# Outer gate tiles of a gated recurrence: the neighbour's three products in one contraction block of 96 rows, and a dot product summed on VectorE

## The reference

```python
xb = xf.reshape(B, L, LRU_BLOCKS, LRU_BLOCK)
r = jax.nn.sigmoid(jnp.einsum('blnc,ncd->blnd', xb, w_a).reshape(B, L, W) + b_a)
i = jax.nn.sigmoid(jnp.einsum('blnc,ncd->blnd', xb, w_x).reshape(B, L, W) + b_x)
log_a = -LRU_C * r * jax.nn.softplus(-lam)
u = jnp.sqrt(-jnp.expm1(2.0 * log_a)) * (i * xf)
```

## Time and profile before

| | us |
|---|---|
| median of three executions (lowest, highest) | 2432.12 (2431.92, 2433.31) |
| the profiled execution's own time | 2431.23 |
| its span, first to last instruction | 2429.4 |
| TensorE busy, share of the span | 2395.8, 99% |
| GpSimd busy | 1727.2, 71% |
| VectorE busy | 1204.4, 50% |
| ScalarE busy | 630.7, 26% |

### The profile page before, as it was taken

How to read it: one execution, slowest core, us unless ns; L and a number is a source line. 1 busy time by engine, 2 the same in 40 slices (tenths; PEclk the granted TensorE clock), 3 DMA queues, 4 the chain that set the end, 5 groups by cost and what they waited for, 6 DMA issues and landing times.

```text
span 2429.4 us, 51213 instructions
## 1 busy us (share of the span) xinstructions
PE 2395.8 (99%) x19460; PEld 2345.1 (97%) x19460; DVE 1204.4 (50%) x1610; ACT 630.7 (26%) x913; POOL 1727.2 (71%) x1970
## 2 busy tenths in 40 slices
PE   7999999999999999999999999999999999999997
PEld 7999999999999999999999999999999999999997
DVE  7665555577754522022366554545786544221222
ACT  2312121326751210011113222221466412100110
POOL 7474757588887777777865756565888877777774
PEclk9999999999999999999999999999999999999998
DMA  5554545322233222322235635453222322223222
GB/s 176 183 187 158 183 155 188 142 96 85 88 100 92 92 92 85 100 86 87 94 130 204 225 140 187 151 183 106 91 92 83 98 97 91 92 84 101 87 86 88
DMA packets 113001, 296.76 MB, mean 122 GB/s; under 512 B 11680, under 2 KB 12448, under 8 KB 112864
## 3 DMA queue, kind: packets, MB, share of 16 engines
q1 hardware_dynamic: 60480, 198.21, 24.9%
q10 hardware_dynamic: 52384, 96.56, 11.4%
HBM read 254.34 MB, written 40.38 MB: 121 GB/s over the span
## 4 chain that ended last, share of the span: by engine, by line
PE 68%; DVE 2%; ACT 1%; DVEq 1%; issue 0%; POOL 0%; ACTq 0%; POOLq 0%
PE banks L395 63%; PE banks L562 1%; PE banks L570 1%; PE banks L531 1%; PE banks L586 1%; PE banks L548 0%; DVE scratch L1095 0%; POOL w_low L381 0%; PE banks L484 0%; DVE ret_acc L1338 0%; DVE scratch L1157 0%; PE banks L442 0%; DVEq L1092 0%; DVE scratch L842 0%; PE banks L540 0%
## 5 line engine op out<-in xcount | busy, mean ns | idle before, releaser
L381 POOL TENSOR_TENSOR w_low<-w_raw,w_high 128x256 fp32r<-128x256 f32 (+1 forms) x1544 | 1285.1, 862 | 61.7
L376 POOL TENSOR_SCALAR w_high<-w_raw 128x1024 fp32r<-128x1024 f32 (+3 forms) x420 | 439.2, 1046 | 619.0 <-PE banks L395 578.0
L395 PE MATMUL banks<-x_high,w_high 128*128 128x260 f32 x4096 | 831.3, 284 | 16.0 <-DVE x_low L749 11.0
L395 PE MATMUL banks<-x_high,w_low 128*128 128x260 f32 x4096 | 825.5, 283 | 0.0
L395 PE MATMUL banks<-x_low,w_high 128*128 128x260 f32 x4096 | 823.5, 283 | 0.0
L395 PEld LDWEIGHTS banks<-x_high,w_high 128*128 128x128 f32 x4096 | 632.2, 189 | 24.5 <-issue 17.0
L395 PEld LDWEIGHTS banks<-x_high,w_low 128*128 128x128 f32 x4096 | 631.3, 188 | 0.0
L395 PEld LDWEIGHTS banks<-x_low,w_high 128*128 128x128 f32 x4096 | 631.0, 188 | 0.0
L395 PE MATMUL banks<-split_scratch,w_high 128*128 128x260 f32 x3776 | 606.9, 282 | 2.1 <-POOL w_low L381 0.9
L395 PEld LDWEIGHTS banks<-split_scratch,w_high 128*128 128x128 f32 x3776 | 517.1, 188 | 3.6 <-ACT split_scratch L1613 1.3
L395 PE MATMUL banks<-split_scratch,w_low 128*128 128x260 f32 x1888 | 380.0, 283 | 0.0
(11 more groups left out here) (170 smaller groups left out, 1926.5 us busy)
## 6 DMA issues: line engine op xcount, KB each, us to landing
w_raw<-in_wstream SPq DMA_DIRECT2D x268, 512.0 KB, 3.5
w_raw<-in_wstream SPq DMA_DIRECT2D x88, 384.0 KB, 3.0
scratch<-in_sret ACTq DMA_DIRECT2D x64, 512.0 KB, 6.8
out_ret_s<-scratch ACTq DMA_DIRECT2D x64, 512.0 KB, 3.5
scratch<-v_rows ACTq DMA_DIRECT2D x64, 256.0 KB, 4.1
w_raw<-in_wstream SPq DMA_DIRECT2D x48, 320.0 KB, 2.8
w_raw<-in_wstream SPq DMA_DIRECT2D x16, 448.0 KB, 3.2
out_ret_p<-scratch ACTq DMA_DIRECT2D x8, 512.0 KB, 2.8
```

What stands on the lines that cost most here:

```text
L376: pool.tensor_scalar(WH[:, j, w], WR[:, j, w], 1.0, 0.0, ALU.mult, ALU.add)
L381: m = pool.tensor_tensor(WL[:, j, p], WR[:, j, p], WH[:, j, p].bitcast(F32), ALU.subtract)
L395: m = pe.matmul(out, wt[:, w, blk * P:(blk + 1) * P], x[xi], start=first and n == 0, stop=last and n == 2)
```

## The change

For outer tiles the neighbour's part of the contraction is at most 32 rows deep (`CR`). ScalarE lays these 32 rows three times into one tile `XS`: high, low, high, 96 rows (`corner`, three copies; one buffer, so it waits for the gates of the outer tile before). The weight block holds the same 32 rows three times, and GpSimd overwrites the third 32 rows of its high part with the low part, so that one block of 96 rows holds high by high, high by low and low by high. TensorE runs it with two matmuls in place of six. The gates wait for `XS` in place of the neighbour tile's low part. GpSimd does this in the second unit of an outer tile, once in each half: drain, copy of 32x128, drain, and the half is reported split only then. In ScalarE's queue the copies stand behind the high part of conv block 3; behind the neighbour copies of turn 0; ahead of the neighbour copies of group 1's tile 1; and behind those of its tile 2.

The dot product's products go into a tile of 16 columns first; a second VectorE instruction adds the two halves into the wide tile, after a drain, and one fp32 matmul is left.

```diff
--- before.py
+++ after.py
@@ -53,6 +53,11 @@
+CR = 32
+OUTER = (0, GT - 1)
...
@@ -151,6 +156,10 @@
 
 
 N_GLX = 2
+
+
+CORNER_UNITS = {B_Y[g][t] + 1 for g in range(GROUPS) for t in OUTER}
+CORNER_BLOCKS = [MT + 2 * w + 1 - YG_UNIT[0] for w in range(2)]
 
 
 PIECE = 2
@@ -202,7 +211,8 @@
         EPST, TOUCH = EPST2[:, 0:1], EPST2[:, 1:2]
         QZ = sb("q_sample", [P, KT, NS * QW])
         VW = sb("v_wide_sb", [P, VT, P])
-        QKW = sb("qk_wide_sb", [P, KT, P])
+        QKW = sb("qk_wide_sb", [P, 1, P])
+        QKP = sb("qk_parts", [P, KT, NS])
         QKD = sb("qk_dot", [P, 1])
         BST = sb("bn_parts", [P, TT + 1, 6])
         MV = sb("mean_var", [P, TT + 1, 2])
@@ -230,6 +240,9 @@
         XNH, XNL = (rview((2 * GT + 2 * i) * TOK, 2, TOK) for i in range(2))
 
         GLH, GLL = (rview((2 * MT - 1 + i * GT) * TOK, GT, TOK) for i in range(2))
+
+        XS = R[:, (2 * GT + 4) * TOK:(2 * GT + 5) * TOK]
+        assert (2 * GT + 5) * TOK <= (2 * MT - 1) * TOK
 
         GL_HI = ([GLH[:, c, :] for c in range(GT)] + [GLX[:, c, :] for c in range(N_GLX)]
                  + [GLH[:, c, :] for c in range(N_GLX, GT)])
...
@@ -380,6 +393,12 @@
                                     p = slice(b * P, min(b + PIECE, b1) * P)
                                     m = pool.tensor_tensor(WL[:, j, p], WR[:, j, p], WH[:, j, p].bitcast(F32),
                                                            ALU.subtract)
+                                for b in CORNER_BLOCKS if base + k in CORNER_UNITS else ():
+                                    if b0 <= b < b1:
+                                        pool.drain()
+                                        c = slice(b * P, (b + 1) * P)
+                                        pool.tensor_copy(WH[2 * CR:3 * CR, j, c], WL[2 * CR:3 * CR, j, c])
+                                        m = pool.drain()
                                 m.then_inc(s["w_split"], 1)
 
 
@@ -523,9 +542,8 @@
                         aux_begin(N_SC + j, hh)
                         if j == TT - 1:
                             pe.wait_ge(s["qk_wide"], hh + 1)
-                            for d in range(KT):
-                                pe.matmul(AUX[:, BANK[N_SC + j], P:P + 1], QKW[:, d, :], ONES[:, 0:1],
-                                          start=d == 0, stop=d == KT - 1)
+                            pe.matmul(AUX[:, BANK[N_SC + j], P:P + 1], QKW[:, 0, :], ONES[:, 0:1],
+                                      start=True, stop=True)
                         for d in range(KT):
                             for n, (a, b) in enumerate(((KH, QH), (KH, QL), (KL, QH))):
                                 m = pe.matmul(AUX[:, BANK[N_SC + j], 0:SEQ - j * P],
@@ -639,11 +657,20 @@
                         n = g * len(INNER) + t - 1
                         pe.wait_ge(s["xn_full"], layer * (GROUPS * len(INNER)) + (n + 1))
                         xs = [pairs(XCH, XCL, t), pairs(XNH, XNL, n % 2)]
-                    else:
-                        pe.wait_ge(s["xc_low"], layer * LT + (g * GT + BAND[t][-1] + 1))
-                        xs = [pairs(XCH, XCL, k) for k in BAND[t]]
+                        for w in range(2):
+                            q = spread(ub0, u, YG_UNIT[t], tb0, idx + 1 + w, xs, q)
+                        return
+                    pe.wait_ge(s["xc_low"], layer * LT + (g * GT + t + 1))
+                    pe.wait_ge(s["xs_full"], layer * (GROUPS * len(OUTER)) + (g * len(OUTER) + OUTER.index(t) + 1))
                     for w in range(2):
-                        q = spread(ub0, u, YG_UNIT[t], tb0, idx + 1 + w, xs, q)
+                        tile_begin(tb0, idx + 1 + w)
+                        outs = [PP[:, slot(idx + 1 + w), c, 0:HALF] for c in range(2)]
+                        b = CORNER_BLOCKS[w]
+                        product(outs, ub0, u + 1, b - 1, pairs(XCH, XCL, t), True, False)
+                        for c in range(2):
+                            m = pe.matmul(outs[c], WH[0:3 * CR, (u + 1) % 2, b * P:(b + 1) * P],
+                                          XS[0:3 * CR, c * HALF:(c + 1) * HALF], start=False, stop=True)
+                        m.then_inc(s["p_done"], 1)
 
                 def lru_out(ub, u, tb, idx):
                     tile_begin(tb, idx)
@@ -980,8 +1007,11 @@
                     ts(KSC[:], KF[:, :, SEQ:TOK], DK ** -0.5, None, ALU.mult)
                     v_tile(0)
                     dve.drain()
-                    tt(wide(QKW[:]), samples(QF), KSC[:].rearrange("p d (j r) -> p d j r", r=ROUNDS),
-                       ALU.mult).then_inc(s["qk_wide"], 1)
+                    tt(QKP[:], QF[:, :, SEQ:TOK], KSC[:], ALU.mult)
+                    dve.drain()
+                    part = QKP[:].rearrange("p d (j r) -> p d j r", r=ROUNDS)
+                    tt(wide(QKW[:]), part[:, 0:1], part[:, 1:2], ALU.add).then_inc(s["qk_wide"], 1)
+                    assert KT == 2
                     low(KL, KF, KH, DK ** -0.5, 2)
                     v_tile(1)
                     if first:
@@ -1613,6 +1643,17 @@
                         m = A(dst[PH:P, n % 2, :], src[PH:P, t - 1, :], copy)
                     m.then_inc(s["xn_full"], 1)
 
+                def corner(g, t):
+
+                    n = g * len(OUTER) + OUTER.index(t)
+                    before = C_RET + MT if n == 0 else C_Y[(n - 1) // 2][OUTER[(n - 1) % 2]] + 3
+                    act.wait_ge(s["p_done"], tb0 + before)
+                    b, r = (t + 1, slice(0, CR)) if t == 0 else (t - 1, slice(P - CR, P))
+                    act.wait_ge(s["xc_low"], layer * LT + (g * GT + b + 1))
+                    A(XS[0:CR, :], XCH[r, b, :], copy)
+                    A(XS[CR:2 * CR, :], XCL[r, b, :], copy)
+                    A(XS[2 * CR:3 * CR, :], XCH[r, b, :], copy).then_inc(s["xs_full"], 1)
+
                 def root(c):
                     act.wait_ge(s["d_full"], layer * LT + (c + 1))
                     A(DF[c % 2], DF[c % 2], ACT.Sqrt).then_inc(s["w_sqrt"], 1)
@@ -1624,6 +1665,8 @@
 
                 for t in range(GT):
                     conv_high(0, t)
+                    if t == GT - 2:
+                        corner(0, 0)
                 for t in range(GT):
                     gates(0, t)
                     if t:
@@ -1633,9 +1676,11 @@
                     if t == 0:
                         neighbours(0, 1)
                         neighbours(0, 2)
+                        corner(0, GT - 1)
                     sig_ga(t)
                     if t == 1:
                         neighbours(0, 3)
+                corner(1, 0)
                 neighbours(1, 1)
                 conv_high(1, GT - 1)
                 gated_high(GT - 1)
@@ -1643,6 +1688,7 @@
                 root(GT)
                 sig_ga(GT)
                 neighbours(1, 2)
+                corner(1, GT - 1)
                 gated_high(GT)
                 gates(1, 1)
                 root(GT + 1)
@@ -1781,14 +1827,16 @@
                 for t in INNER:
                     near[t * P:t * P + PH] = full[(t + 1) * P:(t + 1) * P + PH]
                     near[t * P + PH:(t + 1) * P] = full[(t - 1) * P + PH:t * P]
+                for t, row in ((0, P), (GT - 1, (GT - 1) * P - CR)):
+                    for i in range(3):
+                        near[t * P + i * CR:t * P + (i + 1) * CR] = full[row:row + CR]
                 gates.append((full, near))
             return gates
 
         def y_gates(g, t, gates):
             spread(YG_UNIT[t], [(w_in[l], off[5] + g * wide + t * P, range(MT))]
                    + [b for full, near in gates
-                      for b in ([(full, t * P, [t]), (near, t * P, [t])] if t in INNER
-                                else [(full, t * P, BAND[t])])])
+                      for b in ((full, t * P, [t]), (near, t * P, [t]))])
 
         x_branch(0, 0, X_EARLY)
         ret_out(HEADS - 1)
```

More of the change, by code:

```diff
@@ L55 @@
            for t in INNER)
+CR = 32
+OUTER = (0, GT - 1)
+assert (P - 1) // BLK * BLK + BLK <= P + CR and (GT - 1) * P // BLK * BLK >= (GT - 1) * P - CR
 YG_UNIT = [(MT + 2 * 2) // 2] * GT
@@ L293, in build @@
                  "vs_full vs_st dec_ld trig_ld silu_g t_mul s_new so_mm gn_var gn_sd o_norm sf_full og_full "
-                 "og_high og_low sfin_st sq_mm state_ld xc_full xc_high xc_low xn_full lam_exp gate_i th_full d_full "
+                 "og_high og_low sfin_st sq_mm state_ld xc_full xc_high xc_low xn_full xs_full lam_exp gate_i th_full d_full "
                  "w_sqrt y_gelu gl_full gl_high gl_low small_rd small_st sg_m mg_full mg_high mg_low "
```

## The result

The changed kernel takes 2443.47 us (median; 2442.05 to 2445.35), the kernel before 2431.91 beside it: 11.6 us more, ratio 1.0047 with a 95% interval of 1.0037 to 1.0058. The forecast was 2438.5 and the range ended at 2443.0: the direction came true and the places of the waits did, but the time lies outside the range, 5 us above the forecast. The profiled execution took 2443.76 us with a span of 2442.0, against 2431.23 and 2429.4.

A forecast was written before the change was run, and what follows sets the result against it. TensorE, GpSimd and VectorE were taken to run in one ring, TensorE busiest. Two layers of +4.25 us less 2.1 for the dot product gave +6.4: 2437.6, or 2438.5 on the median's scale; range 2434.0 to 2443.0.

The forecast's parts named there:

- GpSimd's piece: Drain, 32x128 copy and drain in an outer tile's second unit: 0.6 us each, bounds 0.45 to 1.15, 1.2 per tile.
- (c): Layer 0, outer tile 4 of group 0: TensorE's gates end 1.3 us late, and VectorE's merge gate read follows.
- (f): Layer 0, outer tile 4 of group 1: half of the 0.97 us saved is kept, -0.5 us.
- the walk: Layer 0 followed place by place from (a) to (f): +4.25 us, and the same taken for layer 1.
- the matmuls' cut: TensorE's outer tiles: 8 fewer matmuls, 0.97 us less per tile, 7.7 us in all if all of it stays.
- the dot product: One of two fp32 matmuls per head removed from TensorE: 16 x 0.131 = 2.1 us less, all counted.
- (e): ScalarE's queue in group 1, with copies for outer tile 4 in it: TensorE's tile at 648.66 comes 4.75 us late.
- (a): Outer tile 0 of group 0: 0.2 to 0.7 us late, absorbed by the wait at 545.29; 0, perhaps 0.5 in layer 1.
- (b): Copies for outer tile 4 delay merge gate 0's sigmoid: TensorE's x tile at 568.46 +0.95 us, one turn later +1.95.
- (d): Outer tile 0 of group 1: gates begin behind the copies at 631.2, ending 633.1 to 634.2 against 630.32.
- rival 3: GpSimd is dear: each added piece takes 1.2 us because VectorE's work stretches GpSimd's; 2442.7 us, chance 0.13.
- Rival 1: ScalarE's copies vanish at the x tile's slot (568.46) and TensorE keeps its gain: 2422.3, or 2427.4 us; chance 0.06.

The follow-up runs named there:

- e2: Changed kernel without GpSimd's drain, copy and drain: 9.8 us above the kernel before by the median, 7.1 less stretches at the lower clock.
- e6: Kernel before plus ScalarE's three copies per outer tile into an unread spare tile: 13.0 us above before by the median, 10.9 less stretches at the lower clock.
- e1: Kernel before with the dot product's change alone: 2431.16 us, -1.3 against the kernel before.
- e11: Changed kernel with copies moved to ScalarE's idle time and GpSimd's copy and drains replaced by multiplication with a mask block: 8.3 us above the kernel before.
- e4: Changed kernel without GpSimd's drain, copy and drain, and with ScalarE's copies for each layer's first outer tile alone: -1.9 us against the kernel before.
- e3: Changed kernel with ScalarE's three copies for the first outer tile of each layer alone, GpSimd's work kept: 5.5 us above the kernel before.

## Why the prediction was right in direction and 5 us short

The step that failed is GpSimd's piece, in (c) and (f): taken at 0.6 us, with 0.3 of it counted in (c) and half a tile's gain kept in (f), where it is 0.92 and nothing of the gain is left. Beside it the walk kept too much of the matmuls' cut and of the dot product.

Layer 0 step by step; the growth over before is counted from the start of the stage, at the ends of tiles of TensorE (start, for (e)).

- **(a)** forecast 0, or 0.5 in layer 1; found +0.4 in layer 0 and +0.5 in layer 1. The added wait at 545.29 took back less than it could. Without pieces (e2) it is 0.
- **(b)** forecast +1.95; found +2.1 on top of that, at the slot that was named, ended by the merge gate's read (571.63).
- **(c)** forecast: gates 1.3 late, and the same up to (d). Found 2.3 at the gates and 4.7 by the last tile ahead of (d): the waits for the split at 608.63, 613.26 and 620.22. **This step failed.** The forecast gave the piece 0.3 us here; GpSimd had no time left in the units behind it, so both pieces (0.89 and 0.73 us), and a high part of 1.96 us (1.05 at 610.51), all went on.
- **(d)** the gates stand behind the copies, as forecast, and the x tile behind the split (635.95): 4.9 late against 2.8 to 3.9; the extra is (c)'s.
- **(e)** forecast +4.75, found +5.7. As forecast, it hangs on ScalarE's queue, which runs without a gap from the sigmoid (629.86, 2.0 late where (c) had 1.3) to the high part at 651.29; TensorE's own 4.7 to 5.0 lie inside. Without pieces (e2) the place is 5.2 late, against 4.4 by the forecast's own walk without pieces, for the sigmoid was 1.7 late there and not 1.0: VectorE's scan and convolution ahead of it took 1.90 and 3.35 us, 1.61 and 2.80 before. (A stretch at the lower clock in e2, from 632.5 to 635.1, lies beside ScalarE's queue, which has no gap there either, so it is not to be taken off here.)
- **(f)** forecast -0.5; found +0.4. Without pieces (e2) -0.8, most of the 0.97: the pieces again. **This step failed too.**

A stage grew by 6.2 us in layer 0 and 6.7 in layer 1, where 4.25 were forecast. At the end of the first merge gate behind the last gates it is 6.0 and 6.5, and 4.3 and 4.5 without the pieces (e2), where the walk has 4.25 and 3.4. So the pieces bring 1.7 and 2.0 us a layer in place of 0.85, and the copies with the cut 0.9 and 1.1 more than the walk has.

Put as the sum's terms, by the account less stretches: the copies 10.9 (e6; the walk gives 10.7). The cut beside them -2.5 (e2 against e6 and e1: 7.1 - 10.9 + 1.3), where the walk kept -3.9. The pieces on top 4.2 (11.3 - 7.1), where the walk had the remainder, 6.4 - 10.7 + 3.9 + 2.1 = 1.7. The dot product -1.3 instead of -2.1. If e2's stretch beside ScalarE's queue stays in, e2 is 8.3 above before, the cut -1.3 and the pieces 3.0. So the mis-sized terms are **GpSimd's pieces, 1.3 to 2.5 us short**, the cut's kept part, 1.4 to 2.6 too large, and the dot product, 0.8 too large. The first is borne out place by place by (c) and (f); the other two lie within what the account can tell.

The piece was taken at 0.6 us and is 0.92, inside its bounds of 0.45 to 1.15. The copy's 0.3 was no bad price for a copy that starts beside nothing (0.28); what the sum put at nothing is the wait for VectorE's instruction, which ten of 16 copies had and which stands in rival 3 alone. Rival 3 (GpSimd dear, 2442.7, chance 0.13) was the nearest of the cases, with a price too high (1.2 us a piece) and the reason right; the rest of its distance lies in the cut and the dot product.

The medians alone don't bear this out: there the pieces on top of the copies are 1.8 (11.6 - 9.8), which is the forecast's own 1.7, the executions of e2 and of the change overlap, and the copies alone are 13.0. But e2's executions have a mean granted clock of 0.993 to 0.996 and the changed kernel's 0.996 to 0.997: at that place TensorE waits 3.03 us in e2, with a stretch behind it, and 0.52 in the change, where the pieces have made it late already. Among the executions of e2 the time is some 1.4 us shorter for each 0.001 that the mean clock is higher, among those of e11 1.9; at these rates e2 would take some 2439 us at 0.997, the change 2443 (its executions at 0.997), and the pieces on top some 4. That is an estimate from few executions; no run here fixes it.

Of the two rules that the prediction weighed, the rows are against one and for the other. By the Trainium skill, ScalarE: Activation LUTs, section What ACT_TABLE_LOAD costs, a copy would, as an estimate worked out from that page, have cost 0.53 us; the rows of the copies here start 0.65 us apart (549.01, 549.66, 550.31), so for them the measurement decides against it. The other, the Trainium skill, SBUF — State Buffer, section SBUF: two separate sides, has the trace on its side: the same GpSimd copy takes 0.28 us (609.90), or lasts until a VectorE instruction has ended (607.95, 631.42). That the copy waits for that one instruction is shown; that it is by a lock on the ports no run here shows by itself.

Rival 1 (2422.3 to 2427.4) was never near: even with neither the later copies nor the pieces the cut gave 0.6 us. (Its 2427.4 doesn't come out of its own terms either: one tile of four kept in each layer is 1.9 + 2.1 = 4.0 us less, 2428.1.) With the cut at e4's 0.6 us in place of the walk's 3.9, the same sum would have come to 2441.8.

## What to carry to other kernels

Where three engines run in one ring with no time between them, work cut from the busiest is worth what the other two can follow, here 0.6 to 0.8 of 7.7 us, and work added to either of them can cost nearly all of itself: the copies, 15.6 us of ScalarE's time, cost 13.0 by the median when added alone. So ask first what the cut is worth by itself. Price a small GpSimd instruction together with the VectorE instruction that it may start beside (0.28 us alone, up to 1.04 here), not by its share of columns, and look for a place in an in-order queue where an instruction stands behind nothing that anyone waits for: moving the sets of copies took back 4.0 us by the medians, where leaving out three of the four sets a layer gave 6.1 (11.6 - 5.5, e3). Look at the granted clock behind every new wait.

## What the hardware showed that I had not expected

- **The clock falls behind waits.** In the two layers' stages the profiles hold ten stretches with 128x260 matmuls 0.21 us apart, the pace at 1.2 GHz. Each began within 1.5 us behind idle time of TensorE of 1.65 to 3.03 us, had 11 to 17 matmuls at that pace and cost 1.1 to 1.6 us. Not every such wait brings one: the wait of 1.91 us at 571.63 of the changed kernel didn't.
- **Rows.** 96 rows have the price of 128; 64 and 32 rows in turn take 0.21 us at 260 columns (mean 331 and 328 ns against 283).
- **GpSimd.** 128x128 took 0.64 to 0.79 us on average where 128x256 takes 0.86; with a drain between, the end of a copy and the next instruction lie 0.18 us apart ahead of a low part (0.32 in one of eight) and 0.32 ahead of a high part. A copy of 32x128 that starts beside a VectorE instruction on SBUF tensors lasts until 0.09 to 0.15 us behind its end.
